# Seven-product second products in the feed-forward parts of a two-block transformer kernel

## The chip, the cores and the metric

The kernel runs on one core of a Trainium2 chip. The metric is the device time of one execution in microseconds (us).

## What is computed

One sequence of 256 tokens with 1024 features goes through two blocks, all in 32-bit floats. The first has four sub-layers (latent attention, feed-forward, Fourier mixing, feed-forward), the second six (feed-forward, a mixer, feed-forward, twice over). Each of the ten has its own modulation: a row of 3 x 1024 numbers, which is a vector times a 1024 x 3072 matrix and scales, shifts and gates the sub-layer. The change is about the six feed-forward parts:

```
def swiglu(h, w1, w3, w2):          # h 256 x 1024, w1 and w3 1024 x 2816, w2 2816 x 1024
    return (silu(h @ w1) * (h @ w3)) @ w2
...
x = x + g2 * swiglu(rmsnorm(x, norm2_g[i]) * (1 + sc2) + sh2, ffn_w1[i], ffn_w3[i], ffn_w2[i])
```

## The kernel before

Activations lie with features on the 128 partitions: `x` is 8 tiles of 128 x 256, the hidden layer `big` 22 tiles of 128 x 256 (24 in all). One program holds a stream for each engine, and all waits between them are written out as semaphores.

Weights come through a ring of three slots of 128 x 4096, `ring`, filled by the queue of SyncE in the order of a list of phases. A phase has blocks and "units"; a slot is loaded again when TensorE has counted the units of its block (`s_unit`). Beside it runs a ring of three slots, `ada_ring`, for the modulation: 224 blocks of 128 x 1024, loaded by GpSimd's queue (`ada_issue`, L519), each reduced by one VectorE instruction (`ada`, L962). How many VectorE takes at which point is written out: `ADA_IN_UNITS`, `ADA_IN_CHUNKS`, `ADA_IN_RESULTS`. Parts are counted from 0 to 5 (`f`); part 5 has none.

A feed-forward part has three stages. Stage one: the first four hidden tiles by plain products (`raw_unit` or `pairs`). Stage two: nine chunks (`gate_and_up`, `chunk`), each two hidden tiles of gate and up, by Winograd's form of Strassen's method: the features and the tokens are halved, and seven products of 128 tokens x 256 columns replace eight. Activations stand in TensorE, weights move. The sums and differences of h are made once (`combine_h`); two of a chunk's weights are made by GpSimd (`combine`, L528: operations L539 and L540) and two by VectorE (`combine_twice`, L994: L999 and L1001). VectorE adds the products up (`chunk`, L1004: partial_2 and others at L1009, second_gate at L1024, the hidden products at L1020 and L1027), ScalarE does the silu, TensorE turns the two hidden tiles (`turn_hidden`, L1735, four transposes into `pstat`), and ScalarE copies them to `big` (L934).

Stage three, the second products: for each of 8 result tiles m, 22 matmuls of 256 columns, w2 standing, the hidden tile moving, summed in bank `lin[m % 3]`. Tile 0 is in `gate_and_up` (L1781), with the last turn in its midst, the others at the line of `tile_sum` (L1618). VectorE adds each to `x` (`residual`, L1161), in the second block also to a running sum over the tiles (L1166), and takes three modulation blocks (in part 3 two) after each of tiles 0 to 5. The next sub-layer needs the sum or the squares of all eight.

## Time and profile before

| what | value |
| --- | --- |
| runs | 2200.68 us median of 3 (2199.69 to 2203.28) |
| profiled execution | 2197.33 us, span 2195.5 us |
| TensorE busy | 2140.6 us, 97% of the span, mean granted clock 0.99 |
| VectorE, ScalarE, GpSimd busy | 1066.8, 407.0, 374.1 us |
| DMA | 438.41 MB, mean 200 GB/s |
| the nine chunks of part 0 | 113.73 us |
| the second products of part 0 | 76.43 us |

The profile names the engines PE (TensorE), PEld (its weight loads), DVE (VectorE), ACT (ScalarE), POOL (GpSimd) and SP (SyncE). "L1618" is a line of the kernel. A row "out<-in" names the tiles written and read, and a bracket at the end of a row of the timeline says how long the engine had been idle before and who ended that.

### The profile page before, as it was taken

To read this page: it belongs to the slowest core of one execution; us is meant where nothing else is said; L and a number is where in the kernel's file an instruction comes from. 1 tells how busy PE (TensorE), PEld (TensorE's weight loads), DVE (VectorE), ACT (ScalarE), POOL (GpSimd) and SP (SyncE) were. 2 spreads that over 40 slices of the span, in tenths; PEclk is the share of its full clock that TensorE was granted. 3 is DMA by queue.
4 is the path that set the end of the run, shared out by engine and by line. 5 is a ranking of instruction groups with operands and counts; after the bars stand their busy time and mean duration, and the time that the engine had idled before them with its cause. 6 is when DMAs were issued, how large, how long until landed. Compare 5 with 4: busy or idle time off the path is not lost.

```text
span 2195.5 us, 24591 instructions
## 1 busy us (share of the span) xinstructions
PE 2140.6 (97%) x10016; PEld 1803.0 (82%) x10016; DVE 1066.8 (49%) x2111; ACT 407.0 (19%) x775; POOL 374.1 (17%) x339
## 2 busy tenths in 40 slices
PE   7999999989999999999999999999999999999997
PEld 4777888868888888888788888888888868888885
DVE  6545575354663255436433566446644543345412
ACT  3334211022110111023140211021102223121101
POOL 0100243111431143100000044114310000002300
PEclk9999999999999999999999999999999999999998
DMA  9663475874658554743434365656474343434431
GB/s 364 240 259 115 183 274 224 306 267 171 256 217 300 221 228 171 289 177 139 158 117 152 117 268 208 257 206 258 188 266 180 135 153 115 153 125 182 156 123 67
DMA packets 61551, 438.41 MB, mean 200 GB/s; under 512 B 6976, under 2 KB 8768, under 8 KB 39552
## 3 DMA queue, kind: packets, MB, share of 16 engines
q1 hardware_dynamic: 28608, 318.35, 38.1%
q0 software_dynamic: 32256, 117.45, 14.8%
q8 instruction: 79, 1.29, 0.2%
q10 hardware_dynamic: 576, 1.05, 0.1%
q14 instruction: 32, 0.26, 0.0%
HBM read 434.72 MB, written 2.10 MB: 199 GB/s over the span
## 4 chain that ended last, share of the span: by engine, by line
PE 96%; DVE 2%; DMA 1%; ACT 1%; issue 0%; SPq 0%; ACTq 0%; DVEq 0%
PE lin L1618 45%; PE small_ps L1732 17%; PE lin L1732 13%; PE small_ps L1618 4%; PE lin L1781 3%; PE lin L1998 3%; PE lin L1941 1%; DMA ada_ring<-in_ada 1%; PE pstat L1722 1%; PE small_ps L2017 1%; PE lin L1686 1%; PE small_ps L1908 1%; PE lin L1895 1%; PE small_ps L1722 1%; PE small_ps L1989 1%; PE pstat L1630 0%
## 5 line engine op out<-in xcount | busy, mean ns | idle before, releaser
L1618 PE MATMUL lin<-h,ring 128*128 128x256 f32 x1968 | 433.4, 381 | 7.2 <-ACT h L892 2.8
L1618 PEld LDWEIGHTS lin<-h,ring 128*128 128x128 f32 x1968 | 373.0, 191 | 63.4 <-issue 9.1
L1618 PE MATMUL lin<-big,ring 128*128 128x256 f32 x1848 | 399.8, 379 | 0.0
L1618 PEld LDWEIGHTS lin<-big,ring 128*128 128x128 f32 x1848 | 351.1, 190 | 47.7
L974 DVE CUSTOM_DVE_ANT_0 ada_ring<-ada_ring,crow 128x1024 f32<-128x1024 f32 x224 | 265.8, 1220 | 42.6 <-DMA ada_ring<-in_ada 41.8
L539 POOL TENSOR_TENSOR proj<-ring 128x1024 f32<-128x1024 f32 x54 | 127.3, 2357 | 903.0 <-PE small_ps L1618 742.9
L526 POOL DMA_DIRECT2D ada_ring<-in_ada x224 | 120.6, 539 | 811.3 <-DVE sums L974 769.0
L1161 DVE SCALAR_TENSOR_TENSOR x<-lin,mod,x 128x256 f32<-128x256 f32 x80 | 38.5, 483 | 386.4 <-PE lin L1618 322.9
L1732 PE MATMUL small_ps<-ring,h 128*128 128x256 f32 x864 | 195.3, 379 | 0.0
L1732 PEld LDWEIGHTS small_ps<-ring,h 128*128 128x128 f32 x864 | 164.1, 190 | 22.3
L1732 PE MATMUL lin<-proj,sq 128*128 128x256 f32 x672 | 153.8, 379 | 0.0
L1618 PE MATMUL lin<-rec,ring 128*128 128x257 f32 (+1 forms) x608 | 143.1, 386 | 7.8 <-ACT rec L617 7.8
L1732 PEld LDWEIGHTS lin<-proj,sq 128*128 128x128 f32 x672 | 127.7, 190 | 17.4
L1618 PEld LDWEIGHTS lin<-rec,ring 128*128 128x128 f32 x608 | 117.2, 194 | 26.9 <-issue 9.6
L1732 PE MATMUL small_ps<-proj,sq 128*128 128x256 f32 x432 | 105.7, 387 | 0.1
L1732 PE MATMUL small_ps<-ring,sq 128*128 128x256 f32 x432 | 102.2, 379 | 0.0
L1618 PE MATMUL small_ps<-rec,ring 128*128 128x257 f32 x448 | 102.0, 379 | 0.0
L1009 DVE TENSOR_TENSOR att<-lin,att 128x256 f32<-128x256 f32 x108 | 45.8, 424 | 112.0 <-PE lin L1732 111.7
L1732 PEld LDWEIGHTS small_ps<-proj,sq 128*128 128x128 f32 x432 | 78.1, 189 | 21.8 <-issue 13.1
L1618 PEld LDWEIGHTS small_ps<-rec,ring 128*128 128x128 f32 x448 | 84.9, 189 | 12.6
L1732 PEld LDWEIGHTS small_ps<-ring,sq 128*128 128x128 f32 x432 | 78.3, 190 | 8.7
L928 ACT ACTIVATE att<-small_ps 128x256 f32<-128x256 f32 x54 | 20.7, 383 | 328.5 <-PE small_ps L1732 328.4
(335 smaller groups left out, 2344.1 us busy)
## 6 DMA issues: line engine op xcount, KB each, us to landing
ring<-in_w SPq DMA_DIRECT2D x66, 2048.0 KB, 8.3
ada_ring<-in_ada POOLq DMA_DIRECT2D x224, 512.0 KB, 5.6
ring<-in_w SPq DMA_DIRECT2D x48, 1408.0 KB, 6.3
ring<-in_gates SPq DMA_DIRECT2D x12, 2048.0 KB, 8.3
ring<-in_mproj SPq DMA_DIRECT2D x8, 2048.0 KB, 7.6
ring<-in_mtok SPq DMA_DIRECT2D x4, 2048.0 KB, 7.8
ring<-in_branch SPq DMA_DIRECT2D x4, 2048.0 KB, 8.3
ring<-in_wout SPq DMA_DIRECT2D x4, 2048.0 KB, 7.7
```

What stands on the lines that cost most here:

```text
L526: pool.dma_start(ada_ring[n % ADA_SLOTS][:], I["ada"][n]).then_inc(s_ada_dma[n % ADA_SLOTS], 16)
L539: W(combined_weights(j, 0), b12, b11, ALU.subtract).then_inc(s_weights_combined, 1)
L974: V.tensor_tensor_reduce(w, w, crow[:, 0 if s < FIRST2 else 1], 1.0, 0.0, ALU.mult, ALU.add, sums[:, s % 3, b:b + 1]).then_inc(s_ada_used, 1)
L1009: V.tensor_tensor(dst, a, b, ALU.add).then_inc(signal, 1)
L1161: V.scalar_tensor_tensor(x[:, m], lin[(u0 + m) % NBANK][:, 0:T], mod[:, 16 + m:17 + m], x[:, m], ALU.mult, ALU.add).then_inc(s_taken_by_dv ...
L1618: ins = mm(dst, w[:, lo:lo + m], rhs(k), start=k == 0, stop=k == nk - 1)
L1686: ins = mm(lin[i // 2][0:2, i % 2 * T:i % 2 * T + T], csil[:, 0:2, k], first_weights(n)[:, k * T:(k + 1) * T], start=k == 0, stop=k == KD - 1)
L1722: return nc.tensor.transpose(dst, src, ident[:])
L1732: ins = mm(out, activation[:, k], weight[:, :, k * P:(k + 1) * P], start=k == 0, stop=k == 3)
L1781: ins = mm(b[:, 0:T], w[:, k * P:(k + 1) * P], big[:, k], start=k == 0, stop=k == KF - 1)
L1895: mm(lin[n % NBANK][:], q, kh[:, a], start=True, stop=True).then_inc(s_logits, 1)
L1998: ins = mm(b[:], h[:, k, tt * P:tt * P + P], w[:, k * 512:(k + 1) * 512], start=k == 0, stop=k == KD - 1)
```

## The change

The first 768 of the 1024 result columns of stage three are made by the same seven-product form; the last 256 (tiles 6 and 7) stay plain. Now the hidden tiles 2n and 2n+1 are the two halves of the features, and columns 0 to 383 and 384 to 767 of w2 the two halves of the columns. For each of 11 pairs there are seven matmuls with a 128 x 128 hidden tile or sum standing and 384 columns of weights moving. They are summed over all pairs in seven PSUM banks; the result has tokens on the partitions, and TensorE turns it back in 12 transposes.

* w2 comes in six blocks of 2, 2, 1, 2, 2, 2 pairs (`PAIRS`), then two plain ones. Each block is combined like a chunk's: two operations on GpSimd (`combine_result`), two on VectorE (`combine_result_twice`), 384 columns wide per pair. GpSimd starts block b (from 2 on) when TensorE has done block b - 2.
* The hidden pairs need four sums each (`combine_hidden`): those of tiles 0 to 3 are made before chunk 0, those of a turned pair one chunk later, between first_gate and partial_2, from `pstat` and one tile of `big`.
* VectorE adds up the results in seven adds of 384 columns (`results`); the first plain tile waits for the first two of them, the first turn for all.
* The turned tiles are put into `pstat` two at a time, within plain tile 6 (ahead of k = 8, 14, 20), and VectorE adds them to `x` there.
* `keep_modulation` and `fold_gains` move ahead of the combining. The modulation blocks in stage three are 2, 2, 1, 2, 2, 2 beside the blocks, and 4 after tile 5, where they were 3 (in part 3 2) after each of six tiles; the counts in the first stage and the chunks of parts 2 to 4 change to make up for it.

The diff, with the layout of w2 on the host and the semaphores left out:

```diff
-ADA_IN_UNITS = [3, 2, 2, 2, 2, 0]
-ADA_IN_CHUNKS = [[3] * 3 + [2] * 6, [2] * 9, [1] * 9, [2] * 9, [2] * 4 + [1] * 5, [0] * 9]
-ADA_IN_RESULTS = [[3] * 6, [3] * 6, [3] * 6, [2] * 6, [3] * 6, [0] * 6]
+ADA_IN_UNITS = [3, 2, 2, 3, 2, 0]
+ADA_IN_CHUNKS = [[3] * 3 + [2] * 6, [2] * 9, [2] * 3 + [1] * 6, [3] * 2 + [2] * 7, [2] * 7 + [1] * 2, [0] * 9]
+ADA_IN_RESULTS = [[2, 2, 1, 2, 2, 2, 4]] * 5 + [[0] * 7]
+PAIRS = [2, 2, 1, 2, 2, 2]
+HALF = 3 * P
...
-                phase(s, "w2", I["w2"][nf], KD, FF, KD, "d")
+                phase(s, "w2a", I["w2a"][nf], 2, 8 * HALF, 2, "none")
+                phase(s, "w2b", I["w2b"][nf], 1, 4 * HALF, 1, "none")
+                phase(s, "w2c", I["w2c"][nf], 3, 8 * HALF, 3, "none")
+                phase(s, "w2", None, 0, 0, 6, "d")
+                phase(s, "w2d", I["w2d"][nf], 2, FF, 2, "d")
...
+            def combine_result(s, f, b):
+                ph, i = result_block(s, b)
+                n, pairs = ph.first + i, PAIRS[b]
+                if b == 0:
+                    pool.wait_ge(s_fourth_product, f * CHUNKS + CHUNKS - 1)
+                    pool.wait_ge(s_sixth_product, f * CHUNKS + CHUNKS)
+                elif b == 1:
+                    pool.wait_ge(s_fourth_product, f * CHUNKS + CHUNKS)
+                else:
+                    pool.wait_ge(s_result_block, f * len(PAIRS) + b - 1)
+                pool.wait_ge(s_weights[n % SLOTS], (n // SLOTS + 1) * 16)
+                b11, b12, b21, b22 = [result_quarter(n % SLOTS, q, pairs) for q in range(4)]
+                W = nc.gpsimd.tensor_tensor
+                W(combined_result(b, 0, pairs), b12, b11, ALU.subtract).then_inc(s_weights_combined, 1)
+                W(combined_result(b, 2, pairs), b22, b12, ALU.subtract).then_inc(s_weights_combined, 1)
+                ada_issue(ada_before(f) + ADA_IN_UNITS[f] + sum(ADA_IN_CHUNKS[f]) + sum(ADA_IN_RESULTS[f][:b]))
...
+                    act.wait_ge(s_result_first, nth(act, s_result_first))
+                    A(result_kept, product_bank(s, 1, HALF), ACT.Copy).then_inc(s_result_kept, 1)
...
+            def combine_result_twice(s, b):
+                ...
+                dve.wait_ge(s_weights_combined, 2 * made + 1)
+                V.tensor_tensor(t2, result_quarter(slot, 3, PAIRS[b]), t1, ALU.subtract).then_inc(s_weights_combined_twice, 1)
+                dve.wait_ge(s_weights_combined_twice, nth(dve, s_weights_combined_twice))
+                V.tensor_tensor(t4, result_quarter(slot, 2, PAIRS[b]), t2, ALU.subtract).then_inc(s_weights_combined_twice, 1)
+            def combine_hidden(sums4, a11, a12, a21, a22):
+                s1, s2, s3, s4 = sums4
+                V.tensor_tensor(s1, a22, a21, ALU.add).then_inc(s_hidden_combined, 1)
+                V.tensor_tensor(s3, a11, a21, ALU.subtract).then_inc(s_hidden_combined, 1)
+                dve.wait_ge(s_hidden_combined, nth(dve, s_hidden_combined))
+                V.tensor_tensor(s2, s1, a11, ALU.subtract).then_inc(s_hidden_combined, 1)
+                dve.wait_ge(s_hidden_combined, nth(dve, s_hidden_combined, 2))
+                V.tensor_tensor(s4, a12, s2, ALU.subtract).then_inc(s_hidden_combined, 1)
+            def combine_turned_hidden(j):
+                dve.wait_ge(s_hidden_kept, nth(dve, s_hidden_kept))
+                pair = RAW // 2 + j
+                combine_hidden([combined_hidden(pair, n) for n in range(4)], pstat[:, 0:P], pstat[:, T:T + P],
+                               big[:, 2 * pair, P:T], pstat[:, T + P:2 * T])
+            def results(s):
+                f = ffn_before(s)
+                combine_turned_hidden(CHUNKS - 1)
+                for b in range(len(PAIRS)):
+                    if b + 1 < len(PAIRS):
+                        combine_result_twice(s, b + 1)
+                    ada(ADA_IN_RESULTS[f][b])
+                ...
+                added(c11, product(2), result_kept)
+                added(partial, product(6), result_kept)
+                added(c12, product(5), partial)
+                added(c12, product(3), c12)
+                added(c22, product(7), partial)
+                added(c21, product(4), c22)
+                added(c22, product(5), c22)
...
                 V.tensor_tensor(first_gate, product_bank(s, 2), first_kept, ALU.add).then_inc(s_first_gate, 1)
+                if j:
+                    combine_turned_hidden(j - 1)
                 dve.wait_ge(s_sixth_product, nth(dve, s_sixth_product))
...
-                    if name == "w2":
-                        ada(ADA_IN_RESULTS[ffn_before(s)][m] if m < KD - 2 else 0)
+                    if name == "w2" and m == 5:
+                        ada(ADA_IN_RESULTS[ffn_before(s)][-1])
...
                     ada(ADA_IN_UNITS[ffn])
+                    combine_first_hidden(s)
                     for j in range(CHUNKS):
                         chunk(s, j)
                         if j + 1 < CHUNKS:
                             combine_twice(s, j + 1)
+                        else:
+                            combine_result_twice(s, 0)
                         ada(ADA_IN_CHUNKS[ffn][j])
+                    prepare_residual(s)
+                    results(s)
                     residual(s, "w2")
...
-                pe.wait_ge(s_first_up, before + CHUNKS)
-                result(0, 16)
-                turn_hidden(last)
-                result(16, KF).then_inc(s_unit, 1)
+            def results(s):
+                ...
+                pe.wait_ge(s_first_gate, before + CHUNKS)
+                pe.wait_ge(*taken(u13 + RAW - 1))
+                for b, pairs in enumerate(PAIRS):
+                    slot_of(ph, 0, i)
+                    if top >= 2:
+                        pe.wait_ge(s_hidden_kept, before + top - 1)
+                    pe.wait_ge(s_hidden_combined, made + 4 + 4 * max(top - 1, 0))
+                    def part(product, stationary, moving):
+                        out = product_bank(s, product, HALF)
+                        for p in range(pairs):
+                            ins = mm(out, stationary(pair + p), moving[:, p * HALF:(p + 1) * HALF],
+                                     start=b == 0 and p == 0, stop=last and p == pairs - 1)
+                        return ins
+                    ins = part(1, lambda n: big[:, 2 * n, 0:P], b11)
+                    ins = part(2, lambda n: big[:, 2 * n + 1, 0:P], b21)
+                    part(3, lambda n: combined_hidden(n, 3), b22)
+                    if b == 0:
+                        turn_hidden(s, CHUNKS - 1)
+                        pe.wait_ge(s_second_gate, before + CHUNKS)
+                    pe.wait_ge(s_weights_combined, ...)
+                    pe.wait_ge(s_weights_combined_twice, ...)
+                    part(5, lambda n: combined_hidden(n, 0), t1)
+                    part(6, lambda n: combined_hidden(n, 1), t2).then_inc(s_unit, 1)
+                    ins = part(7, lambda n: combined_hidden(n, 2), t3)
+                    part(4, lambda n: big[:, 2 * n + 1, P:T], t4).then_inc(s_result_block, 1)
+                for m in (6, 7):
+                    w = slot_of(ph, 0, m - 6)
+                    pe.wait_ge(s_result_added, 7 * f + (2, 7)[m - 6])
+                    for k in range(KF):
+                        if m == 6 and k in (8, 14, 20):
+                            turn_results((k - 8) // 6)
+                        ins = mm(lin[(u + m) % NBANK][:, 0:T], w[:, k * P:(k + 1) * P], big[:, k], start=k == 0, stop=k == KF - 1)
+                    ins.then_inc(s_unit, 1)
```

## Rows read from the trace of the kernel before

**Rows 1.** The page: the chain that ended last, its share of the span by engine.
```profile
PE 96%; DVE 2%; DMA 1%; ACT 1%; issue 0%; SPq 0%; ACTq 0%; DVEq 0%
```
**Rows 2.** Stretches of part 0: window, length, busy by engine, clock, DMA, GB/s.
```profile
255.34:369.07 113.73, 113.63 (x538) 98.14 (x537) 76.42 (x144) 14.88 (x35) 49.36 (x38) 1.00 0.67 262
369.07:445.50 76.43, 76.43 (x357) 67.29 (x357) 27.63 (x51) 2.91 (x5) 10.60 (x20) 1.00 0.77 284
```
**Rows 3.** The chain in order of time: start, length, engine, line, instructions.
```profile
271.32 3.59 PE small_ps L1732 x16
...
379.00 66.48 PE lin L1618 x308
...
1762.22 6.87 PE lin L1998 x16
...
1781.45 7.06 PE lin L1998 x16
```
**Rows 4.** Instructions of a line: durations in ns, min, median, max.
```profile
L1618 PE MATMUL lin<-big,ring x1848: 379/379/379, 378.8 to 2176.2; 128*128 128x256 f32 x185
...
L1823 PE MATMUL lin<-ring,proj x24: 486/486/987, 78.8 to 88.0; 128*128 128x384 f32 x24
...
L1998 PE MATMUL lin<-ring,h x128: 592/592/697, 1037.9 to 1797.8; 128*128 128x512 f32 x128
```
**Rows 5.** Groups by line and shape: count, busy us, mean ns.
```profile
L539 POOL TENSOR_TENSOR proj<-ring 128x1024 f32<-128x1024 f32 x54 | 127.3, 2357 | 903.0 <-PE small_ps L1618 742.9 <-issue 111.7 <-PE lin L1618 30.6
...
L999 DVE TENSOR_TENSOR proj<-ring,proj 128x1024 f32<-128x1024 f32 x54 | 65.6, 1215 | 0.0
...
L1485 DVE TENSOR_TENSOR bias<-bias 128x128 f32<-128x128 f32 x2 | 0.5, 288 | 9.4 <-DMA work<-in_relb 9.4
```
**Rows 6.** Timeline of chunks of part 0: start, length, engine, line.
```profile
264.02 0.42 DVE L1009 TENSOR_TENSOR att<-lin,att 128x256 f32<-128x256 f32 x1 [2.51 <-PE lin L1732]
...
287.67 1.22 DVE L974 CUSTOM_DVE_ANT_0 ada_ring<-ada_ring,crow 128x1024 f32<-128x1024 f32 x1
...
288.82 0.08 DVE L974 DVE_READ_ACCUMULATOR2_ANT sums<- 128x1 f32 x1
...
289.34 0.42 DVE L1009 TENSOR_TENSOR att<-lin,att 128x256 f32<-128x256 f32 x1
289.74 2.36 POOL L539 TENSOR_TENSOR proj<-ring 128x1024 f32<-128x1024 f32 x1
...
292.86 0.42 DVE L1024 TENSOR_TENSOR att<-lin,att 128x256 f32<-128x256 f32 x1 [1.37 <-PE lin L1732]
...
294.80 0.41 ACT L931 ACTIVATE att<-att 128x256 f32<-128x256 f32 x1
...
352.99 0.42 DVE L1009 TENSOR_TENSOR att<-lin,att 128x256 f32<-128x256 f32 x1 [1.25 <-PE lin L1732]
```
**Rows 7.** Timeline of VectorE and GpSimd ahead of part 1's chunks.
```profile
525.63 0.47 DVE L1566 SCALAR_TENSOR_TENSOR big<-rec,small,sil 128x256 f32<-128x256 f32 x1
...
528.35 1.15 DVE L1566 SCALAR_TENSOR_TENSOR big<-rec,small,sil 128x256 f32<-128x256 f32 x1 [0.65 <-ACT sil L916]
...
529.18 2.52 POOL L540 TENSOR_TENSOR proj<-ring 128x1024 f32<-128x1024 f32 x1
```
**Rows 8.** DMA issues: part 0's second products, then the page; KB, us to landing.
```profile
ada_ring<-in_ada POOLq DMA_DIRECT2D x20, 512.0 KB, 5.8
...
ada_ring<-in_ada POOLq DMA_DIRECT2D x224, 512.0 KB, 5.6
```
**Rows 9.** The chain in order of time, in the Fourier part.
```profile
477.57 4.18 DMA ada_ring<-in_ada
...
483.30 8.88 DMA ada_ring<-in_ada
```
**Rows 10.** Timeline of VectorE at the end of part 2.
```profile
941.45 0.42 DVE L1166 TENSOR_TENSOR rstd<-rstd,x 128x256 f32<-128x256 f32 x1
950.50 0.48 DVE L1161 SCALAR_TENSOR_TENSOR x<-lin,mod,x 128x256 f32<-128x256 f32 x1 [8.62 <-PE lin L1618]
```

More of the change, by code:

```diff
@@ L68 @@
 CHUNKS = KF // 2 - RAW // 2
+PAIRS = [2, 2, 1, 2, 2, 2]
+HALF = 3 * P
+HIDDEN_SUMS = 4 + 4 * CHUNKS
 SLOTS = 3
@@ L288, in build @@
         phases, takes, unit0, unit_end = [], [], {}, []
-        count = {"a": 0, "d": 0}
+        count = {"a": 0, "d": 0, "none": 0}
         def phase(s, name, src, nb, width, units, taker):
             first = phases[-1].first + phases[-1].nb if phases else 0
-            phases.append(Phase((s, name), src, nb, width, first, len(takes), units // nb))
-            unit_end.extend(len(takes) + (b + 1) * (units // nb) for b in range(nb))
+            per = units // nb if nb else 0
+            phases.append(Phase((s, name), src, nb, width, first, len(takes), per))
+            unit_end.extend(len(takes) + (b + 1) * per for b in range(nb))
             unit0[s, name] = len(takes)
@@ new lines, in combine_first_hidden @@
+            def combine_first_hidden(s):
+                dve.wait_ge(*taken(unit0[s, "w13"] + RAW - 1))
+                sums4 = [yab[:].rearrange("p (n a) b -> p n (a b)", n=2)[:, :, n * P:(n + 1) * P] for n in range(4)]
+                tiles = big[:, 0:4].rearrange("p (n a) b -> p n a b", n=2)
+                combine_hidden(sums4, tiles[:, :, 0, 0:P], tiles[:, :, 1, 0:P], tiles[:, :, 0, P:T], tiles[:, :, 1, P:T])
+            def combine_turned_hidden(j):
[3 more added lines that the diff above has]
+                               big[:, 2 * pair, P:T], pstat[:, T + P:2 * T])
@@ L1722, in turn, with turn_hidden @@
                 return nc.tensor.transpose(dst, src, ident[:])
+            def turn_hidden(s, j):
+                f = ffn_before(s)
+                pe.wait_ge(*taken(unit0[s, "w13"] + RAW + 2 * j + 1))
+                if j:
+                    pe.wait_ge(s_hidden_kept, f * CHUNKS + j)
+                    pe.wait_ge(s_hidden_combined, f * HIDDEN_SUMS + 4 + 4 * j)
+                for a in range(2):
+                    for tt, tokens in enumerate((first_up, second_gate)):
+                        at = a * T + tt * P
+                        ins = turn(pstat[:, at:at + P], tokens[:, a * P:(a + 1) * P])
+                ins.then_inc(s_hidden_turned, 1)
             def gate_and_up(s):
@@ L1733, in part @@
                     return ins
-                def turn_hidden(j):
-                    pe.wait_ge(*taken(u0 + RAW + 2 * j + 1))
-                    if j:
-                        pe.wait_ge(s_hidden_kept, before + j)
-                    for a in range(2):
-                        for tt, tokens in enumerate((first_up, second_gate)):
-                            at = a * T + tt * P
-                            ins = turn(pstat[:, at:at + P], tokens[:, a * P:(a + 1) * P])
-                    ins.then_inc(s_hidden_turned, 1)
                 h_tile(KD - 1)
@@ L1770, in gate_and_up @@
                     part(4, quarter_of_h(1, 1), t4).then_inc(s_fourth_product, 1)
-                last = CHUNKS - 1
-                ph = by_name[s, "w2"]
-                w = slot_of(ph, 0, 0)
-                b = bank(ph.unit0)
-                def result(k0, k1):
-                    for k in range(k0, k1):
-                        if k >= RAW and k % 2 == 0:
-                            pe.wait_ge(s_hidden_kept, before + (k - RAW) // 2 + 1)
-                        ins = mm(b[:, 0:T], w[:, k * P:(k + 1) * P], big[:, k], start=k == 0, stop=k == KF - 1)
-                    return ins
@@ L2170, in _ @@
                     gate_and_up(s)
-                    ph = by_name[s, "w2"]
-                    for m in range(1, KD):
-                        w = slot_of(ph, m // SLOTS, m % SLOTS)
-                        tile_sum(bank(ph.unit0 + m)[:, 0:T], w, 0, KF, lambda k: big[:, k]).then_inc(s_unit, 1)
+                    results(s)
                 if kind == "mix":
```

118 lines of the change are left out of this document (106 added, 12 removed).

## The prediction

> **What bounds the kernel now.** I read the page first, its chain that ended last: 96% of it is TensorE's own work [rows 1]. Then the stretches of one feed-forward part: the nine seven-product chunks last 113.73 us with 113.63 busy, the second products 76.43 with 76.43 busy, where VectorE has 27.63 and GpSimd 10.60 [rows 2]. So a column taken from TensorE is time, as long as nothing new makes it wait. The chain in order of time prices it: 308 half products of 256 columns in 66.48 us, 0.2159 each; 16 of 512 columns in 6.87, 0.4294 each, in another place 7.06 [rows 3]. (A product of 32-bit numbers is two such instructions.) The second products are 8 x 22 x 2 = 352 halves, 76.00 us, and one turn of a hidden pair: by what is left of 76.43 [rows 2], 0.43.
>
> **TensorE after the change.** 768 columns: 11 pairs x 7 products x 2 = 154 halves of 384 columns, a width that this stage hasn't. Midway between 256 and 512 it is 0.3226 us; the single durations of 379, 486 and 592 ns for 256, 384 and 512 rise by equal steps too, and the 384 form of the trace has weights moving and activations standing, as here [rows 4]. 154 x 0.3226 = 49.69. The two plain tiles: 2 x 22 x 2 x 0.2159 = 19.00. Turns: the last hidden pair and three groups of results, four transposes each, 4 x 0.43 = 1.72. In a chunk, behind a turn and product 3, three waits stand ahead of product 5, and those 16 halves take 3.59 instead of 3.45 [rows 3]: 0.14, once per part. The plain tiles' two waits cost nothing in the 66.48, so I give the other joints of blocks nothing. Sum 70.55, a gain of 5.88 per part, 35.3 for six. Bounds: 0.14 at every joint, 11 more, is 1.5 per part, 9 in all; halves that stretch as in the 7.06 row (0.012 x 154), 11 in all.
>
> **What is added elsewhere, and what hides it.** Below, t is the time since TensorE left the last chunk. It wants product 5 of blocks 0 to 5 at t = 4.4, 13.5, 20.6, 27.0, 36.0, 45.1 and ends them at 50.3 (each matmul 0.645, a block of two pairs 9.03).
>
> *Sums of the hidden tiles.* Four VectorE adds of 128 columns per chunk. One of 128 took 288 ns [rows 5]; overlapped, with two dependent waits, about 1.1 us, at most four of 256 (0.42), 1.7. They stand before partial_2. VectorE idles 1.25 us there in a chunk with two modulation blocks and not at all in one with three, and in both 1.37 behind the five adds [rows 6]. The fourth add has two SBUF inputs, and the trace shows what that can do: L1566's product, 0.47 us at 525.63, took 1.15 at 528.35 while GpSimd was at its combining, and GpSimd's next one 2.52 [rows 7]. With two blocks the adds end 0.4 before GpSimd starts. With three (behind the first three chunks of part 0 and, newly, the first two of part 3) the fourth starts behind GpSimd's start at 289.74 and is held until 292.1: second_gate comes 1.5 us late, at 294.4 for 292.86 [rows 6]. Its silu would run on ScalarE at 294.80 anyway, behind the copy of the next product 1, so the second hidden product moves by under 0.1, and the turn can stand 0.3. Nothing, therefore; without this cover five chunks would pay 1.5 each, 7.5 us. The four first sums of a part (four of 256, 1.7) fall in the 2.51 us idle of chunk 0 [rows 6].
>
> The Trainium skill, "SBUF — State Buffer", section "Who interferes with whom", has this as a rule, and it speaks against this change, which sets VectorE's and GpSimd's combining side by side: a VectorE instruction with two SBUF inputs and a GpSimd instruction that reads SBUF exclude each other for the whole instruction. The trace agrees (1.15 for 0.47 [rows 7]). Without the rule block 3 below would be 1.8 us early, and the sum 1 us better.
>
> *Combining the weights.* GpSimd takes 2357 ns for 1024 columns, so 1.77 for 768; VectorE 1215, so 0.95 [rows 5]. GpSimd makes block 0 between the sixth product of the last chunk (t = -3.3) and 0.4, VectorE from 1.4 to 3.3: 1.1 before it is wanted. From then on there is a serial loop: VectorE's two operations 1.9; two modulation blocks 2.3 (one every 1.15 [rows 6]); 0.84 from the last one's end to GpSimd's next combine, with the DMA's issue between (288.90 to 289.74 [rows 6]); GpSimd's two 3.54, which hold VectorE. That is 8.6, against 9.03 of TensorE. Played through: GpSimd is at block 1 from 6.6 to 10.2, VectorE ready at 12.4 (wanted 13.5); block 2, half as wide, GpSimd 15.5 to 17.3, ready 18.4 (20.6); block 3, 21.5 to 25.1, ready 27.0 (27.0); block 4, ready 34.1 (36.0); block 5, ready 42.5 (45.1). Parts 2 and 4 have one modulation block behind the last chunk and run 1.15 earlier, part 5 none. Block 3, behind the short block, is the tight one: 0.3 us of stall in parts 0, 1 and 3, 1 us; bounds 0 and 3.
>
> *The result sums.* After block 5 VectorE has four modulation blocks in a row, with three slots: the fourth's DMA is issued at t = 44.0, once the first is used. Its landing is a median of 5.8 us in part 0's second products and 5.6 over the kernel [rows 8]; in the Fourier part one landed in 4.18, and one in 8.88 as lines of weights came in beside it [rows 9]. The load of weights beside this one (issued 38.7) ends at 45, so I take 4.6, near the low end: the block ends at 49.8, then come two adds of 384 columns (0.56 each, on the line from 0.42 for 256 to 1.22 for 1024) before TensorE may start the first plain tile: 50.95 for 50.3, 0.65 late in parts 0, 1 and 3, nothing in 2 and 4. 2 us; at 4.2 nothing to 1, at 5.6 1.65 x 3 + 0.5 x 2 = 6. The other five adds end within 3 us of that, the first turn comes 3.45 after the tile's start, and the second turn wants two residual steps, under 2 us, and gives them 2.6.
>
> *The end of the part.* Before, no modulation block follows tile 5, and step 7 finds VectorE idle for 8.62 us [rows 10]. Now four stand between step 5 and step 6: third turn over at 60.4, two steps with the running sum (0.48 + 0.42 and their gaps [rows 10], 0.98 each), first block at 62.3, the fourth's DMA issued 1.5 later, landed 5.6 later (the median [rows 8], since a load of weights runs beside it), block 1.15, step 6 at 70.6, step 7 at 71.6 instead of 70.7. So 0.9 in parts 2, 3 and 4; in parts 0 and 1, which have no running sum, step 6 is done 0.7 before it matters. 2.8 us; 0 at 4.6, and at 8.9 4.2 x 3 + 2.6 x 2 = 18.
>
> *At nothing:* the bytes are the same, 1536 KB per 9.0 us beside up to 1 MB of modulation, some 290 GB/s where the stage moved 284 [rows 2]; ScalarE, idle there, has one copy more; keep_modulation and the gains move ahead of the blocks, 0.2 to 1 us, in the played times above; the next part's first load is asked for at t = 47.7, earlier than before.
>
> **Sum.** 35.3 - 1 - 2 - 2.8 = 29.5. The profiled execution took 2197.33 us with a span of 2195.5; the median of the runs, 2200.68, is 3.35 above it. I carry the difference over: 2200.7 - 29.5 = 2171.2, a profiled execution of 2168.
>
> **Rivals.**
> 1. *All hidden*: the modulation blocks land within 4.6 us or less and block 3 is in time: 2200.7 - 35.3 = 2165.4. For it the 4.18 [rows 9]; against it the medians [rows 8]. 0.22.
> 2. *The wider products or the joints cost more*: the change gives less than its count says. 9 to 11 us, with the forecast's stalls 2180 to 2182. Against it the equal steps [rows 4]. 0.10.
> 3. *Late modulation blocks*: a landing of 5.6 everywhere loses 1 + 6 + 2.8 = 10, 2175.5; each further us costs some 13 (five parts at the result sums, five at the end, three at block 3), so 7 gives 2193. 0.13.
> 4. *Slower, by the same queue*: VectorE, in its fixed order, sits on a modulation DMA while TensorE waits for its adds; the place is the fourth block in a row, twice per part. It decides at 35.3 us lost, a landing of 7.6; at the 8.88 of [rows 9] each time the loss is about 54, 2219. The medians speak against it. 0.05.
> The forecast, 2168 to 2175, has 0.50.
>
> The range goes from a little below rival 1, 2163, to 2186, which takes in rival 2 and the nearer half of rival 3. A measurement of this kernel tells about 0.2%, 4.4 us, from no change. Faster 0.95, the same 0.01, slower 0.04.
>
> **What would show it.** Second products in 71 to 73 us; halves of 384 columns every 0.323; VectorE waiting for in_ada ahead of the result sums and of step 6; TensorE waiting for a result sum at the first plain tile and for VectorE's combine at block 3, and hardly elsewhere; chunks still 12.66 apart. It is wrong if chunks lengthen (the held fourth add is passed on), if every block waits for its weights, or if a turn of results costs far more than 0.43.

## Result and profile after

| | before | after |
| --- | --- | --- |
| median of the runs, us | 2200.35 (2199.69 to 2203.28, 4 runs) | 2188.12 (2186.85 to 2189.53, 4 runs) |
| ratio | | 0.9942 [0.9925, 0.9959] |
| profiled execution, its span | 2197.33, 2195.5 | 2189.53, 2187.7 |
| mean granted clock of TensorE | 0.990 | 0.983 |

The kernel is 12.2 us faster. 29.5 were forecast, and 2188.1 lies above the range of 2163 to 2186. The two profiled executions are 7.8 us apart, since that of before was 3 us faster than its median and that of after 1.4 slower; the accounts below are made between profiles. In them the kernel before looks a little better than it is: its profiled execution has a mean granted clock of 0.990, its executions in the jobs of the experiments 0.986 to 0.989, and on the whole they are the slower the lower it is (2198.11 us at 0.989, 2205.23 at 0.986).

First the stretches of part 0 in the kernel after (the columns are those of [rows 2]):

```profile
core 0: us, PE busy (x) PEld busy (x) DVE busy (x) ACT busy (x) POOL busy (x), PEclk, DMA share, GB/s
254.99:368.38 113.39, 113.39 (x537) 98.22 (x536) 84.78 (x180) 14.92 (x35) 52.54 (x40) 1.00 0.67 264
368.38:439.22 70.84, 70.84 (x260) 47.55 (x259) 44.95 (x66) 3.40 (x6) 25.43 (x27) 1.00 0.73 268
```

The second products have gone from 76.43 to 70.84, where 70.55 were worked out. So the change does what it says, and the question is what is lost elsewhere. I split the span at three marks in each part (first product of the chunks, first of the second products, last plain matmul), from TensorE's rows:

| sum over the parts, us | before | after | e2 | e9 | e12 |
| --- | --- | --- | --- | --- | --- |
| six chunk stages | 680.5 | 680.7 | 680.6 | 680.3 | 680.2 |
| six second products | 459.5 | 432.8 | 431.3 | 423.7 | 423.7 |
| from part 0 to part 1 (the Fourier part) | 95.05 | 96.28 | 98.59 | 99.66 | 92.94 |
| between parts 1, 2, 3, 4 and 5 | 686.4 | 703.9 | 688.4 | 688.6 | 690.8 |
| of the last row, TensorE's clock at 1.2 GHz | 13.7 | 37.5 | 17.1 | 17.1 | 17.1 |

In the kernel after, the six second products take 70.84, 74.29, 71.96, 72.85, 70.86 and 71.98; where nothing makes them wait (four of the six in e9, below) they take 70.58 each. So TensorE's work shrank by 35.9 us, 9.3 are lost again within the stage, and 18.7 behind it: 17.5 between parts 1 to 5, 1.2 in the Fourier part. The groups of instructions by line name a part of this (busy and mean ns of one, then the idle time ahead of them and who ended it):

```profile
L1995 PE MATMUL lin<-big,ring 128*128 128x256 f32 x528 | 118.3, 380 | 2.3 <-DVE tok L1123 2.3
L1962 PE MATMUL small_ps<-ring,big 128*128 128x384 f32 x264 | 91.0, 486 | 0.0
L1962 PE MATMUL small_ps<-proj,xc 128*128 128x384 f32 x48 | 18.8, 495 | 3.1 <-DVE proj L1085 2.7 <-DVE tok L1085 0.4
L1962 PE MATMUL small_ps<-proj,yab 128*128 128x384 f32 x24 | 8.8, 490 | 1.2 <-DVE tok L1085 1.2
L2387 PE MATMUL small_ps<-rstd,ones 128*128 128x256 f32 x12 | 4.6, 469 | 13.9 <-DVE rstd L1316 13.9
```

The 384-column products have the 486 ns of [rows 4]. L1995 are the plain tiles: 2.3 us for the result sums. L1962 are the new products: 2.7 and 1.6 us for VectorE's combine. The brackets count too little, since a matmul's record runs on for some 0.16 us after the next could start. From start to start of the matmuls, less what the columns take, all 9.3 us are found: 5.2 for the combine, 3.0 for the result sums (0.13, 0.90, 1.18 and 0.76 in parts 0 to 3), and 1.1 in joints of under 0.12 each. The matmul for the mean (L2387), which comes behind step 7, waited 6.6 us before and waits 13.9 now.

**The end of part 3**, in order of time (start, duration, then what; the bracket is the idle time before and who ended it):

```profile
1434.35 10.53 PE L1995 MATMUL lin<-big,ring 128*128 128x256 f32 x48
1438.11 0.53 POOL L577 DMA_DIRECT2D ada_ring<-in_ada  x1 [14.04 <-DVE sums L1047]
...
1438.87 1.22 DVE L1047 CUSTOM_DVE_ANT_0 ada_ring<-ada_ring,crow 128x1024 f32<-128x1024 f32 x1
...
1445.31 1.22 DVE L1047 CUSTOM_DVE_ANT_0 ada_ring<-ada_ring,crow 128x1024 f32<-128x1024 f32 x1 [5.21 <-DMA ada_ring<-in_ada]
...
1447.43 0.48 DVE L1311 SCALAR_TENSOR_TENSOR x<-lin,mod,x 128x256 f32<-128x256 f32 x1
...
1448.52 1.19 PE L2387 MATMUL small_ps<-rstd,ones 128*128 128x256 f32 x2 [3.65 <-DVE rstd L1316]
...
1451.63 6.72 PE L1773 MATMUL lin<-rec,ring 128*128 128x257 f32 x16 [1.91 <-ACT rec L688]
```

The same place in the kernel before:

```profile
1452.59 0.48 DVE L1161 SCALAR_TENSOR_TENSOR x<-lin,mod,x 128x256 f32<-128x256 f32 x1 [8.62 <-PE lin L1618]
...
1453.59 0.70 PE L2180 MATMUL small_ps<-rstd,ones 128*128 128x256 f32 x2 [1.11 <-DVE rstd L1166]
...
1455.84 3.72 PE L1618 MATMUL lin<-rec,ring 128*128 128x257 f32 x16 [1.55 <-ACT rec L617]
```

The reader is to see two things. TensorE is done at 1444.88, and step 7 starts 2.55 us later instead of 0.11: VectorE sat on the fourth modulation block. The chain of waits gives the transfer:

```profile
1437.82 0.28 issue
1438.11 7.18 DMA ada_ring<-in_ada
```

It landed 7.18 us after its issue; parts 0, 1, 2 and 4 have 7.82, 7.66, 7.10 and 6.79. And the 16 matmuls behind the idle took 6.72 instead of 3.72. The granted clock in windows, after and before (PEclk is the third figure from the end):

```profile
1450.00:1455.00 5.00, 3.37 (x8) 2.77 (x9) 2.48 (x4) 4.03 (x10) 0.00 (x0) 0.50 0.58 241
1455.00:1460.00 5.00, 5.00 (x18) 4.08 (x18) 1.92 (x2) 2.64 (x4) 0.00 (x0) 0.73 0.00 0
```

```profile
1455.00:1460.00 5.00, 4.16 (x19) 3.69 (x20) 1.88 (x4) 4.82 (x12) 0.00 (x0) 1.00 0.80 344
1460.00:1465.00 5.00, 5.00 (x24) 4.36 (x24) 2.48 (x3) 2.90 (x5) 0.00 (x0) 1.00 0.00 0
```

Around an idle of 3.65 us and another of 1.91, TensorE fell to its lower level, 1.2 GHz (the fall came within the first: the two matmuls between them took 1.19 us for 0.70), where it kept 2.4 with 1.11 and 1.55. Read alike in all parts, step 7 (in parts 0 and 1 the last of steps 6 and 7) is 1.3, 1.2, 2.4, 2.4 and 2.1 us later, 9.4 in all. 8.1 of them lie between parts 1 and 5, where 17.5 are lost; the other 9.4 I put down to the clock, to be tested.

**Part 1's second products** are the longest, 74.29. Four rows of them:

```profile
666.60 0.54 POOL L577 DMA_DIRECT2D ada_ring<-in_ada  x1 [3.27 <-issue]
...
668.20 1.34 DVE L1083 TENSOR_TENSOR proj<-ring,proj 128x384 f32<-128x384 f32 x1 [4.60 <-POOL proj L608]
...
670.28 0.88 PE L1962 MATMUL small_ps<-proj,xc 128*128 128x384 f32 x2 [0.43 <-DVE tok L1085]
...
678.80 1.53 PE L1962 MATMUL small_ps<-proj,xc 128*128 128x384 f32 x4 [1.84 <-DVE proj L1085]
```

GpSimd was idle for 3.27 us ahead of its 114th modulation transfer (number 113, counted from 0), and the last of that with nothing to wait for ("issue"): the transfer starts 3.00 us after VectorE has freed its slot, and its neighbours in the queue start 0.31 after it. So the pause is 2.7 us. Its combine of block 2 came late, and the loop passed this on: TensorE waits 0.43 at block 2 and 1.84 at block 3. The kernel before had a pause ahead of the same transfer, in its second products, where no other engine waited for GpSimd (the 9.81 hold the wait for a free slot too; here as well the transfer starts 3.00 us behind VectorE's release):

```profile
659.70 1.06 POOL L526 DMA_DIRECT2D ada_ring<-in_ada  x2 [9.81 <-issue]
```

**Part 5** has a wait of its own:

```profile
2097.06 1.81 POOL L608 TENSOR_TENSOR proj<-ring 128x768 f32<-128x768 f32 x1
2098.26 1.43 DVE L1083 TENSOR_TENSOR proj<-ring,proj 128x768 f32<-128x768 f32 x1
2098.82 2.53 POOL L609 TENSOR_TENSOR proj<-ring 128x768 f32<-128x768 f32 x1
2099.72 2.45 DVE L1085 TENSOR_TENSOR tok<-ring,proj 128x768 f32<-128x768 f32 x1
...
2102.31 1.53 PE L1962 MATMUL small_ps<-proj,yab 128*128 128x384 f32 x4 [1.18 <-DVE tok L1085]
```

With no modulation transfer to issue, GpSimd began block 1 while VectorE was still to combine block 0; VectorE's two operations took 1.43 and 2.45 us, and TensorE waited 1.18.

### The profile page after: what moved, and what is told of

The parts are those of the page before. It is cut to its first block, busy times and chain, and to the rows that moved or that the text cites. A ratio compares the mean times of both kernels' runs of the same rounds, so it can differ in the third digit from the quotient of the medians.

```text
span 2187.7 us, 23955 instructions
## 1 busy us (share of the span) xinstructions
PE 2118.1 (97%) x9428; PEld 1691.0 (77%) x9428; DVE 1256.4 (57%) x2465; ACT 410.9 (19%) x781; POOL 495.8 (23%) x411
## 3 DMA queue, kind: packets, MB, share of 16 engines
q0 software_dynamic: 32256, 117.45, 15.2%
## 4 chain that ended last, share of the span: by engine, by line
PE 85%; DVE 6%; DMA 4%; POOL 2%; issue 2%; ACT 1%; SPq 0%; ACTq 0%; DVEq 0%; POOLq 0%
PE lin L1773 27%; PE small_ps L1900 17%; PE lin L1900 13%; PE small_ps L1773 4%; PE small_ps L1962 4%; DMA ada_ring<-in_ada 4%; PE lin L1962 3%; PE lin L1995 3%; PE lin L2208 3%; DVE ada_ring L1047 2%; PE pstat L1877 1%; PE lin L2151 1%; DVE proj L1083 1%; PE small_ps L2227 1%; POOL proj L608 1%
## 5 line engine op out<-in xcount | busy, mean ns | idle before, releaser
L1773 PE MATMUL lin<-rec,ring 128*128 128x257 f32 (+1 forms) x608 | 150.2, 400 | 8.1 <-ACT rec L688 8.1
L1773 PEld LDWEIGHTS lin<-rec,ring 128*128 128x128 f32 x608 | 122.2, 202 | 29.7 <-issue 10.3
L1995 PE MATMUL lin<-big,ring 128*128 128x256 f32 x528 | 118.3, 380 | 2.3 <-DVE tok L1123 2.3
L1995 PEld LDWEIGHTS lin<-big,ring 128*128 128x128 f32 x528 | 98.5, 190 | 17.8 <-issue 5.2
L1083 DVE TENSOR_TENSOR proj<-ring,proj 128x768 f32<-128x768 f32 (+1 forms) x36 | 69.0, 1917 | 74.1 <-POOL proj L608 74.1
L1962 PE MATMUL small_ps<-ring,big 128*128 128x384 f32 x264 | 91.0, 486 | 0.0
```

The source lines that it names most:

```text
L1083: V.tensor_tensor(t2, result_quarter(slot, 3, PAIRS[b]), t1, ALU.subtract).then_inc(s_weights_combined_twice, 1)
L1773: ins = mm(dst, w[:, lo:lo + m], rhs(k), start=k == 0, stop=k == nk - 1)
L1962: ins = mm(out, stationary(pair + p), moving[:, p * HALF:(p + 1) * HALF], start=b == 0 and p == 0, stop=last and p == pairs - 1)
L1995: ins = mm(lin[(u + m) % NBANK][:, 0:T], w[:, k * P:(k + 1) * P], big[:, k], start=k == 0, stop=k == KF - 1)
```

## Experiments

All edits are to the kernel after, except e4. Ratios are to the kernel before, run in the same job; its medians in the five jobs were 2200.35, 2201.62, 2200.66, 2202.17 and 2201.73.

**e1_tail3**: three modulation blocks after tile 5.

```diff
-ADA_IN_RESULTS = [[2, 2, 1, 2, 2, 2, 4]] * 5 + [[0] * 7]
+ADA_IN_RESULTS = [[2, 2, 1, 2, 2, 2, 3]] * 5 + [[0] * 7]      # ADA_IN_CHUNKS: one more per part
```

> Three modulation blocks instead of four after tile 5, so that none waits for a slot to be refilled; one more per part in a chunk. Theory A (step 7 comes 10.0 us late in parts 0 to 4 because of the fourth block's DMA, and the longer idle of TensorE then brings stretches at half clock worth 8.9): all of both comes back, 2188.1 - 18.9 = 2169. Theory B (the half clock comes from the narrower flow of the new stage, not from the lateness): 2178, with the stretches of half clock still there. Theory C (the transitions are longer because the steps of tiles 0 to 5 are now bunched ahead of ScalarE's and VectorE's work for the next part): under 5 us, 2184 or more.

Measured: 2181.07, 0.9899 [0.9878, 0.9919], none of the three forecasts. Step 7 is on time in all parts (0.04 to 0.11 us behind TensorE's end), and between parts 1 to 5 the sum fell from 703.9 to 692.8. It is still 6.4 above that of before, with 27.3 us at 1.2 GHz. And part 1's second products took 78.00. GpSimd's pause is the same 2.7 us, but it stood ahead of transfers 113 and 114 together; VectorE then waited for the first of them, GpSimd's combine of block 3 for VectorE, and TensorE for both, and 6.8 us at half clock followed:

```profile
667.95 1.10 POOL L577 DMA_DIRECT2D ada_ring<-in_ada  x2 [5.96 <-issue]
...
675.95 1.23 DVE L1047 CUSTOM_DVE_ANT_0 ada_ring<-ada_ring,crow 128x1024 f32<-128x1024 f32 x1 [2.77 <-DMA ada_ring<-in_ada]
...
683.56 2.90 PE L1962 MATMUL small_ps<-proj,xc 128*128 128x384 f32 x4 [4.69 <-DVE proj L1085]
```

**e2_spread**: four blocks still, but one after tile 1, one after tile 3, two after tile 5.

```diff
-                    if name == "w2" and m == 5:
-                        ada(ADA_IN_RESULTS[ffn_before(s)][-1])
+                    if name == "w2" and m in (1, 3, 5):
+                        ada(ADA_IN_RESULTS[ffn_before(s)][-1] * (1, 0, 1, 0, 2)[m - 1] // 4)
```

> The four blocks taken as 1 after tile 1, 1 after tile 3, 2 after tile 5: the same four in the same stage, but the refill of the first slot is asked for some 6 us earlier. Theory A: as the run with three, 2169 to 2171, since step 6 is then done several us before step 7. Theory B: 2178. Theory C: 2184 or more. If VectorE's extra 1.15 us between the turns makes TensorE wait there: up to 5 us above A.

Measured: 2176.09, 0.9887 [0.9867, 0.9906], between theory A's 2169 to 2171 and theory B's 2178; the trace decides. Step 7 starts 0.04 to 0.11 after TensorE's end in all parts, 15.5 of the 17.5 us between parts 1 to 5 are back (688.4), and so is the clock (17.1 us at 1.2 GHz for 37.5). The number of the blocks is not the cause, their place is.

**e3_fill**: the late step stays, TensorE is kept busy.

```diff
                     ins.then_inc(s_unit, 1)
+                if 0 < f < 5:
+                    for k in range(5):
+                        mm(pa[1][:, 0:T], ident[:], big[:, k], start=True, stop=True)
```

> Five matmuls of 256 columns (2.16 us) into a free bank behind tile 7 of parts 1 to 4, where TensorE waits 2.9 to 3.7 us; the result is unused. The lateness of step 7 stays. Theory A: the half clock in the transitions of parts 1 to 4 goes, the 10 us of lateness stay: 2188.1 - 7 to 9 = 2179 to 2181, mean clock 0.989. Theory B: no change, or slower, 2188 or more.

Measured: 2182.07, 0.9918 [0.9897, 0.9939], 1 us above the 2179 to 2181 of theory A. TensorE at the end of part 3:

```profile
1439.65 2.32 PE L1999 MATMUL small_ps<-big,ident 128*128 128x256 f32 x10
1442.85 0.67 PE L2390 MATMUL small_ps<-rstd,ones 128*128 128x256 f32 x2 [0.88 <-DVE rstd L1316]
1445.42 5.14 PE L1773 MATMUL lin<-rec,ring 128*128 128x257 f32 x16 [1.91 <-ACT rec L688]
```

The idle of 3.65 is 0.88, and the 16 matmuls take 5.14 instead of 6.72. Between parts 1 to 5 the sum is 695.0, 8.9 less. Step 7 is also 1.1 us less late over the four places, so 7.8 of it came with the clock (17.1 us at 1.2 GHz for 37.5), with most of the lateness left in. So some 7.8 of the 9.4 us put down to the clock were the clock; the rest is not shown.

**e4_before_late**: the lateness alone, in the kernel before.

```diff
-ADA_IN_RESULTS = [[3] * 6, [3] * 6, [3] * 6, [2] * 6, [3] * 6, [0] * 6]
+ADA_IN_RESULTS = [[3, 3, 3, 3, 2, 0, 4]] * 3 + [[2, 2, 2, 2, 0, 0, 4], [3, 3, 3, 3, 2, 0, 4], [0] * 7]
...
-                        ada(ADA_IN_RESULTS[ffn_before(s)][m] if m < KD - 2 else 0)
+                        ada(ADA_IN_RESULTS[ffn_before(s)][m] if m < KD - 1 else 0)
```

> The kernel before, with plain second products, but four modulation blocks after tile 6 (fewer after tiles 4 and 5; the same number per part). Theory A: step 7 is 1 to 2.5 us late in parts 0 to 4 here too and half-clock stretches follow: 2200.4 + 8 to 19 = 2208 to 2219. Theories B and C: 2200 to 2208 without more half clock, or no change.

Measured: 2210.19, 1.0036 [1.0025, 1.0048], 8.6 us above the median of the kernel before. Between the profiles the sum of the stretches behind the parts rose by 13.1 us; step 7 is 6.4 us later over the parts, and the time at 1.2 GHz between parts 1 to 5 went from 13.7 to 34.1. The loss needs nothing of the seven-product form.

**e5_f5_wait**: GpSimd waits for VectorE's block 0.

```diff
                     pool.wait_ge(s_fourth_product, f * CHUNKS + CHUNKS)
+                    pool.wait_ge(s_weights_combined_twice, 2 * (f * (CHUNKS + len(PAIRS)) + CHUNKS + 1))
```

> In the second products GpSimd's combine of block 1 also waits until VectorE has made its two sums of block 0. Nothing else is changed. Theory: the wait of TensorE at the first block of part 5 (1.18 us at 2102.31, released by VectorE's combine L1085) is there because GpSimd, which in this part has no modulation DMAs to issue, starts block 1 at once and locks VectorE out of its two-input instruction: VectorE's two operations took 1.43 and 2.45 us instead of 0.95. Then part 5's second products go from 71.98 to about 70.8, with both operations at 0.95, and parts 0 to 4 stay within 0.3 us, since GpSimd comes later than VectorE there anyway. Rival: VectorE's operations are slow because of what they read (PSUM or ring traffic), or TensorE waits for the weights' DMA; then the wait stays at about 1.2 us.

Measured: 2186.43 in one run, too little for a ratio; the stage is read from its trace. Part 5's second products took 70.59:

```profile
2096.58 0.95 DVE L1084 TENSOR_TENSOR proj<-ring,proj 128x768 f32<-128x768 f32 x1
2097.57 0.96 DVE L1086 TENSOR_TENSOR tok<-ring,proj 128x768 f32<-128x768 f32 x1
...
2099.30 1.46 PE L1963 MATMUL small_ps<-proj,yab 128*128 128x384 f32 x4
```

As expected, 1.4 us. Parts 0 to 4 moved by -0.8 to +1.1, more than the 0.3 that I gave: their waits differ from run to run.

**e6_no_overlap**: VectorE waits for both of GpSimd's operations.

```diff
-                dve.wait_ge(s_weights_combined, 2 * made + 1)
+                dve.wait_ge(s_weights_combined, 2 * made + (2 if b else 1))
```

> In the second products VectorE's combine of blocks 1 to 5 waits for both of GpSimd's operations of the block instead of the first alone. Theory (the two engines exclude each other): VectorE's L1083 in these blocks goes from about 2.5 to 0.95 us, the end of each pair of VectorE operations stays where it was to within 0.3 us, and the second products stay at 432.8 +- 1.5 in all: the wait costs nothing, because the overlap never existed. Rival (they run side by side and VectorE is slow for its own reasons, such as width or memory traffic): the operations stay at about 2.5 and start 1.7 us later, the serial loop of 8.6 us becomes 10.3 against TensorE's 9.03, and the second products grow by 1 to 2 us at each of blocks 2 to 5, 20 to 50 us over the kernel.

Measured: 2195.32, 0.9973 [0.9964, 0.9982]; second products 435.9. Block 1 of part 0, after and then e6:

```profile
375.05 1.82 POOL L608 TENSOR_TENSOR proj<-ring 128x768 f32<-128x768 f32 x1
376.82 1.82 POOL L609 TENSOR_TENSOR proj<-ring 128x768 f32<-128x768 f32 x1
376.90 2.56 DVE L1083 TENSOR_TENSOR proj<-ring,proj 128x768 f32<-128x768 f32 x1 [1.44 <-POOL proj L608]
379.49 0.96 DVE L1085 TENSOR_TENSOR proj<-ring,proj 128x768 f32<-128x768 f32 x1
```

```profile
375.69 1.82 POOL L608 TENSOR_TENSOR proj<-ring 128x768 f32<-128x768 f32 x1
377.46 1.81 POOL L609 TENSOR_TENSOR proj<-ring 128x768 f32<-128x768 f32 x1
379.31 0.96 DVE L1083 TENSOR_TENSOR proj<-ring,proj 128x768 f32<-128x768 f32 x1 [3.20 <-POOL proj L609]
380.30 0.96 DVE L1085 TENSOR_TENSOR proj<-ring,proj 128x768 f32<-128x768 f32 x1
```

VectorE starts 1.85 us after GpSimd in the one and 3.62 after it in the other, and yet its second operation ends 5.40 and 5.57 us after GpSimd's start. The overlap does not exist: VectorE's 2.56 us are 1.6 of standing and 0.96 of work. The rival's 20 to 50 us did not come. The wait costs 0.17 per block; the stage is 3.1 us longer, more than the 1.5 that I allowed, and how much of it is this wait isn't shown, since parts move by up to 1.1 from run to run (e5). The median is 7 us up and the profile's span only 2.8: most of the other executions have a mean granted clock of 0.981 or 0.982, the profiled one 0.983. The Trainium skill, "SBUF — State Buffer", section "Who interferes with whom", says that a VectorE instruction with two SBUF inputs contends with a GpSimd instruction that reads SBUF, and that the lock is exclusive. The trace agrees: 1.6 of VectorE's 2.56 us were standing.

**e7_spread_more**: e5's wait, 2, 1, 1, 2, 2, 1 beside the blocks, and more behind the tiles.

```diff
+ADA_IN_RESULTS = [[2, 1, 1, 2, 2, 1, 6]] * 5 + [[0] * 7]
...
+                    if name == "w2" and ffn_before(s) < 5:
+                        ada((0, 1, 0, 1, 0, 2, 2, 0)[m])
```

> As e2_spread, with e5's wait, and the modulation blocks of parts 0 to 4 at 2, 1, 1, 2, 2, 1 beside the blocks and then 1 after tile 1, 1 after tile 3, 2 after tile 5 and 2 after tile 6. No place has more than three in a row, so VectorE never sits on a transfer that was only just asked for. Theory (late modulation blocks plus the half clock that follows the longer idle of TensorE): the result sums' waits (1.9 to 2.9 us on VectorE, 0.6 to 1.0 on TensorE in parts 1, 2 and 3) go, block 2's and 3's stall shrink, part 5 wins 1.2: 3 to 5 us off e2_spread's 2176, so 2171 to 2173, with the second products at 426 to 428 and the stretches between at 796. Rival: two blocks after tile 6 make step 7 late again by 1 to 2 us in each part, and it ends at e2_spread's 2176 or above.

Measured: 2184.13, 0.9922 [0.9909, 0.9936]. The second products fell to 425.5, all at 70.6 to 70.9 but part 1's, 72.24. But the rival was right on the tail, and larger than it said: VectorE waited for the second block behind tile 6, step 7 came 2.0 to 2.9 us after TensorE's end, and the clock followed (704.8 between parts 1 to 5, as in the kernel after).

**e8_pause_moved**: as e7, with five blocks of part 1 moved to its chunks.

```diff
-[2] * 9,                  # ADA_IN_CHUNKS, part 1
+[3] * 5 + [2] * 4,
```

> As e7_spread_more, but in part 1 five modulation blocks are taken in the chunks (3 after each of the first five) instead of in the second products, so that number 113 of GpSimd's transfers, ahead of which GpSimd paused for 3.3 to 6 us in every run so far, is asked for in the chunks. If the pause belongs to this number of the queue, part 1's second products have none and come to about 71 us (74.3 in the changed kernel), some 2 us off e7, and the chunk stage hides it, since a late transfer there is not wanted for 10 us. If the pause belongs to the place in the program (the instructions of part 1's first or second result block) or to the time near 660 us, it stays in the second products.

Measured: 2179.80, 0.9903 [0.9888, 0.9918]. The pause went with the number of the transfer:

```profile
637.00 2.35 POOL L590 TENSOR_TENSOR proj<-ring 128x1024 f32<-128x1024 f32 x1 [1.15 <-issue]
649.53 1.10 POOL L577 DMA_DIRECT2D ada_ring<-in_ada  x2 [7.87 <-issue]
```

It is transfers 113 and 114 again, 3.00 us behind the release of the first one's slot, now at 649.5 behind the last chunk's combine, where nobody needs GpSimd; part 1's second products took 70.57, 1.7 less than in e7. All six together are 423.8. The edit did a second thing: part 1 has four blocks behind its tiles instead of six, its step 7 is on time (0.04 for 2.02 us), and the way to part 2 is 3.4 us shorter.

**e9_both**: e8's second products with e2's tail (behind tiles 1, 3 and 5: 1, 1, 2), the other two blocks in the chunks, and e5's wait.

```diff
+ADA_IN_CHUNKS = [[3] * 5 + [2] * 4, [3] * 5 + [2] * 4, [2] * 5 + [1] * 4, [3] * 4 + [2] * 5, [2] * 9, [0] * 9]
+ADA_IN_RESULTS = [[2, 1, 1, 2, 2, 1, 4], [1, 1, 1, 1, 1, 1, 4]] + [[2, 1, 1, 2, 2, 1, 4]] * 3 + [[0] * 7]
...
+                    if name == "w2" and ffn_before(s) < 5:
+                        ada((0, 1, 0, 1, 0, 2, 0, 0)[m])
```

> e8_pause_moved's second products with e2_spread's tail: nothing after tile 6, one modulation block after tile 1, one after tile 3, two after tile 5; the two blocks that stood behind tile 6 go to the chunks. Theory (two separate losses that add up: waits inside the second products, and the late step 7 with the half clock behind it): second products at 423.8 as in e8, stretches between at about 797 as in e2, in all 7 to 8 us off e2's 2176: 2168 to 2170. Rival: with the second products in time the tail is reached earlier, the blocks after tile 5 find their transfers not landed, and step 7 is late again: 2174 or more.

Measured: 2167.97, 0.9845 [0.9832, 0.9859]. Second products 423.7, 688.6 between parts 1 to 5: the two losses add up, as expected. (With the marks of the table the stretches between are 787.0 in e2 and 788.3 here, the Fourier part with them, and not the 797 of the expectation; the two are alike, as it says.)

**e10_none_behind**: as e9, but no block behind the tiles, up to 26 in a part's chunks.

> No modulation block behind the result tiles at all; up to 26 of a part's go to the chunks, three per chunk. Theory: step 7 of every part is as early as in the kernel before, the idle of TensorE at the end of the parts is the 1.1 to 2 us that it was, and the stretches between are at 791 to 797; 2163 to 2168 if chunks with three blocks eight times in a row hide them as the three to five of part 0 and 1 did. Rival: VectorE idles not at all in a chunk with three, so lateness piles up over eight of them and the chunks lengthen by 0.3 to 1 us each: chunk stages of 114 to 120 us in parts 0, 1, 3, and a time above e9's.

Measured: 2169.64, 0.9855 [0.9840, 0.9870]. Chunks with three blocks eight times in a row cost part 1 0.9 us (114.30) and the others up to 0.1; nothing was won at the tail over e9 (690.1 between parts 1 to 5). It is above the theory's 2163 to 2168, and 1.7 above e9, where the executions of either spread over 2 to 4 us. Of the rival's longer chunks only part 1 shows some.

**e11_both_fill**: e9 with e3's filling matmuls.

> e9_both with e3's five unused matmuls behind tile 7 of parts 1 to 4. Theory: the half clock goes only where an idle of over 3 us is left at the end of a part; if e9 has brought these back to the length of the kernel before, little of it is left, and the fill gives 0 to 3 us. Rival: the clock falls there whatever the length of the idle; then it gives the 9 us of e3 again, 2160.

Measured: 2165.38, 0.9838 [0.9825, 0.9852]: 2.6 us below e9, within the spread of the two, and not the 8.9 of e3. Between parts 1 to 5 the time at 1.2 GHz went from 17.1 to 10.2 us, and the sum from 688.6 to 687.5. So most of what the fill gave in e3 came with the long idle.

**e12_fewer_in_fourier**: e11 with 15 blocks in the Fourier part and three more in part 0's chunks.

```diff
-ADA_IN_FOURIER = 18
+ADA_IN_FOURIER = 15
```

> As e11_both_fill, with 15 modulation blocks in the Fourier part instead of 18 and three more in the chunks of part 0. Theory: since the first second products end earlier, TensorE waits in the Fourier part for VectorE, which waits for modulation transfers one after the other (from 448 to 488 us the chain goes through five of them and the last takes over 9 us in every run): the stretch from the end of part 0 to the next chunk is 95.05 us in the kernel before and 98 to 100 in the better variants, so some 4 us of the gain are given back there. Each block takes about 2.2 us of that chain, and three fewer bring the stretch to 93 to 95: 2159 to 2162. Rival: the wait there is for the Fourier part's weights and the late block only fits in beside them; then the last block is as late, and the time stays at 2165 +- 2.

Measured: 2162.67, 0.9824 [0.9810, 0.9837], the fastest, between the theory's 2159 to 2162 and the rival's 2165. The chain of waits in the Fourier part, e9 and then e12:

```profile
472.13 5.60 DMA ada_ring<-in_ada
...
479.28 9.50 DMA ada_ring<-in_ada
...
491.06 22.70 PE lin L1774 x96
```

```profile
460.72 14.10 PE lin L2177 x64
...
474.84 0.60 ACT h L635
...
475.49 31.37 PE lin L1774 x144
```

In e9 the chain ran through five modulation transfers, the last of 9.50 us; in e12 through none, and the stretch is 92.94 us, below every other run's. The kernel before has the same five in its chain, the last of 8.88 [rows 9], and 95.05 us; the kernel after has 96.28, with 0.3 from the late step 7 of part 0, and e9 99.66. Of e9's 4.6 us, 1.7 are half clock behind the long wait (96 matmuls in 22.70 us for 21.01). How long the five take differs from run to run: e3, which is the kernel after up to this place, has 98.59. In e12 3.2 us were lost again between parts 1 to 5 (690.8 for 687.5 in e11), with 17.1 us at 1.2 GHz for 10.2.

## Why the prediction missed

* *TensorE's work*: right. 70.55 worked out, 70.58 measured without waits; six times 5.99 instead of 5.88, 35.9 for 35.3. The halves of 384 columns, the turns of 0.43 and the joints of blocks were priced well; rival 2 falls.
* *Sums of the hidden tiles*: right. The chunk stages are 680.7 for 680.5; the held fourth add is not passed on.
* *Result sums*: the size is near, 2 us forecast and 2.3 measured (3.0 from start to start), but the places show luck in it. Parts 2 and 4 were to run 1.15 us earlier and lose nothing; in part 2 the fourth block was asked for at 44.2 us, as in part 0 (44.1), and part 2 lost most, 1.18, where part 0 lost 0.13 for 0.65. The landing was priced well here: 3.8 to 4.9 us in the five parts, for 4.6.
* *Combining the weights*: under-sized, 1 for 4.3 us of waits (2.7 and 1.6), 5.2 from start to start. 0.9 of it is block 3 of part 3, the place that was named, with 0.3; parts 0 and 1 have nothing of this kind. 2.3 come from GpSimd's pause in part 1, which [rows 7] and [rows 8] did not show, but which stood in the trace of before; 1.2 is part 5, which the prediction left out since it has no modulation blocks. That was wrong: the blocks also hold GpSimd back until VectorE is through.
* *The end of the part*: the step that failed. The wait was seen, but it was sized at 2.8 us over the parts and measured 9.4. It took the landing for 5.6, the median, and it was 6.8 to 7.8. Parts 0 and 1 were given nothing because they have no running sum, and were 1.3 and 1.2 late (of part 0's only 0.3 came through to the next product). A median was a poor guide: the 224 transfers of the kernel after landed in 3.7 to 13.9 us, 88 of them in over 7.
* *What the prediction did not have at all*: the clock. The idle of TensorE grew from 1.11 to 3.65 us, and half clock came with it; 9.4 us, as much as the lateness itself, of which e3 shows some 7.8. It was put at nothing, and no reason was given.
* *The sum*: 35.9 - 9.3 - 18.7 is 7.9 between the two profiles, where their spans differ by 7.8. The forecast's stalls of 5.8 us are 28 there, and 24 between the medians, since the profiled execution of before had a higher clock than most.

Rival 3 had the mechanism (late modulation blocks), but charged each us of landing at thirteen places. The late landing was at the end of the part only, and beside it stood the clock, which no rival had; so a landing near the 7.6 of rival 4 did not make the kernel slower, but the way between the parts cost 18.7 us. e2, e3 and e4 show this, each from another side; e9 and e12 show that with both losses away the kernel has 2168.0 and 2162.7, below the forecast of 2171. Not settled: what GpSimd's pause is; that it belongs to the number of the transfer rests on e8 to e12, where the transfer was moved, and on its place in all fourteen traces. Nor is it settled why part 3's second idle is 1.91 us in the new form and 1.55 before, with half clock (e9) and without it.

## What to carry to other kernels

Where an engine in a fixed order waits for a transfer that was only just asked for, price the landing from the rows of that very place and not from a median, and count as many blocks as slots between two results that TensorE wants: the last one more than that is the one that costs. When a change lengthens an idle of TensorE by a few us, look at the granted clock behind it, for the loss can double. And look in the chain of the kernel before for waits on a queue that the change doesn't touch (the Fourier part's five transfers here): they can be worth as much as the change loses.

## What the runs showed of the hardware

* Number 113 of GpSimd's 224 transfers, counted from 0, starts 3.00 us after its slot is free in all fourteen traces, at times from 635 to 669 us; the others, from the fourth on, start within 0.7 us of the later of two things, their slot's release and the end of GpSimd's work before. What is special about it is open. Each transfer is 144 packets (32256 in all), so by an estimate with even shares 1017 packets for each of the 16 DMA engines lie ahead of it; no run changes that number.
* A transfer of 512 KB on GpSimd's queue beside a load of weights on SyncE's landed after 6.8 to 7.8 us at the ends of the five parts, and after 9.4 and 9.5 in the Fourier part (477.76 in the kernel after, 479.28 in e9); the other four in those two chains took 4.5 to 5.9, with a median of 5.7 over the kernel after.
* Idle times of 1.20 and 1.91 us, in e9, still brought 5.40 us for the 16 matmuls that took 3.72 behind 1.11 and 1.55, and the same two idles 6.53 in e1: how much clock is lost behind the same place is not fixed.
* VectorE's subtract of 768 columns with two SBUF inputs took 2.56 us beside GpSimd's 1.82 us operation and 0.96 behind it (e6). GpSimd can be the one that stands: 2.53 us for 1.82 in part 5.
